# Top-k of a product-key layer: the sums over one-hots move from VectorE to GpSimd, a head behind

## The reference, cut to what matters

```python
s = jnp.einsum('phsd,hsnd->phsn', qry, p['peer_subkeys']).astype(jnp.float32)
s1, i1 = lax.top_k(s[:, :, 0], PEER_TOPK)
s2, i2 = lax.top_k(s[:, :, 1], PEER_TOPK)
cand = (s1[..., :, None] + s2[..., None, :]).reshape(PEER_BLOCK, PEER_HEADS, PEER_TOPK * PEER_TOPK)
cidx = (i1[..., :, None] * PEER_NKEYS + i2[..., None, :]).reshape(PEER_BLOCK, PEER_HEADS, PEER_TOPK * PEER_TOPK)
top_s, pos = lax.top_k(cand, PEER_TOPK)
idx = jnp.take_along_axis(cidx, pos, axis=-1)
gates = jax.nn.softmax(top_s, axis=-1)
```

## Time and profile before

| | |
|---|---|
| median of 3 runs | 4236.36 us (4228.61 to 4244.34) |
| profiled execution, its own time | 4242.22 us |
| its span | 4240.3 us |
| busy over the span | TensorE 3691.2 us (87%), VectorE 3024.4 (71%), ScalarE 1471.0 (35%), GpSimd 2050.7 (48%) |
| mean granted TensorE clock | 0.953 |

### The profile page before, as it was taken

One profiled execution on the slowest core, in us unless ns is written; L12 is line 12 of the kernel. 1 busy time (PEld: TensorE's weight loads), 2 busy tenths in 40 slices (PEclk: granted clock), 3 DMA queues, 4 the chain that ended last, 5 costly groups with the idle time before them and its releaser, 6 DMA issues. The chain is left out here.

```text
span 4240.3 us, 66262 instructions
## 1 busy us (share of the span) xinstructions
PE 3691.2 (87%) x24298; PEld 3423.3 (81%) x24298; DVE 3024.4 (71%) x4791; ACT 1471.0 (35%) x1882; POOL 2050.7 (48%) x1144
## 2 busy tenths in 40 slices
PE   6876999999997898997679999999999898898986
PEld 3335988888896797997578888999898888888886
DVE  4777655566655214898978777778878888888886
ACT  5665444434442113222332332333332322223222
POOL 2333222222224233334047676777777767676772
PEclk9997999999998898998999999999999999999998
DMA  7991222222222123222589999999999999999994
GB/s 301 347 345 66 87 81 85 75 81 79 75 66 100 53 101 114 74 78 92 174 317 401 397 415 396 402 408 418 414 401 405 412 396 418 403 409 416 406 413 169
DMA packets 256208, 1090.68 MB, mean 257 GB/s; under 512 B 25352, under 2 KB 78856, under 8 KB 176392
## 3 DMA queue, kind: packets, MB, share of 16 engines
q1 hardware_dynamic: 170512, 543.60, 34.6%
q0 software_dynamic: 73728, 536.90, 30.9%
q10 hardware_dynamic: 11776, 7.52, 0.6%
HBM read 1047.54 MB, written 40.40 MB: 257 GB/s over the span
## 5 line engine op out<-in xcount | busy, mean ns | idle before, releaser
L248 POOL TENSOR_TENSOR wlo<-raw,whi 128x1024 fp32r<-128x1024 f32 x551 | 1344.4, 2443 | 1333.5 <-ACT whi L244 1328.2
L244 ACT CAST whi<-raw 128x1024 fp32r<-128x1024 f32 x670 | 699.1, 1049 | 1285.2 <-DMA raw<-in_u 535.1
L2099 PE MATMUL gps<-chi,whi 128*128 128x320 f32 x2048 | 656.7, 321 | 110.5 <-DVE outacc L2228 80.9
L263 PE MATMUL gps<-hi_d,whi 128*128 128x320 f32 x2048 | 653.2, 319 | 92.7 <-DVE wlo L253 61.9
L2099 PE MATMUL gps<-chi,wlo 128*128 128x320 f32 x2048 | 645.8, 315 | 0.0
L2099 PE MATMUL gps<-clo,whi 128*128 128x320 f32 x2048 | 645.7, 315 | 0.0
L263 PE MATMUL gps<-lo_d,whi 128*128 128x320 f32 x2048 | 643.6, 314 | 0.0
L263 PE MATMUL gps<-hi_d,wlo 128*128 128x320 f32 x2048 | 643.2, 314 | 0.0
L2186 DVE SCALAR_TENSOR_TENSOR dps<-ring,coef,dps 128x2048 f32<-128x2048 f32 x252 | 591.8, 2348 | 4.7 <-DVE dps L2186 0.9
L2173 DVE CUSTOM_DVE_ANT_0 ring<-ring,dps 128x2048 f32<-128x2048 f32 x256 | 582.2, 2279 | 0.0
L280 PE MATMUL gps<-act_hi,whi 128*128 128x288 f32 x2080 | 477.2, 311 | 37.9 <-POOL act_lo L511 9.0
(11 more groups left out here) (384 smaller groups left out, 5906.6 us busy)
## 6 DMA issues: line engine op xcount, KB each, us to landing
raw<-in_u SPq DMA_DIRECT2D x256, 512.0 KB, 10.5
raw<-in_v SPq DMA_DIRECT2D x256, 512.0 KB, 8.6
wada<-in_w_ada SPq DMA_DIRECT2D x96, 1024.0 KB, 6.6
raw<-in_w_in SPq DMA_DIRECT2D x96, 512.0 KB, 3.4
gateD<-gst SPq DMA_DIRECT2D x8, 2560.0 KB, 9.9
gate<-gateD SPq DMA_DIRECT2D x32, 640.0 KB, 13.5
raw<-in_w_out SPq DMA_DIRECT2D x32, 512.0 KB, 3.7
raw<-in_w_q SPq DMA_DIRECT2D x32, 512.0 KB, 3.8
```

The lines of the kernel that those rows point to most:

```text
L244: act.copy(whi[:, k.slot, :], raw_of(k)).then_inc(W.hi, 1)
L248: pool.tensor_tensor(wlo[:, k.slot, :], raw_of(k), whi[:, k.slot, :].bitcast(F32), ALU.subtract).then_inc(W.lo, 1)
L263: m = pe.matmul(gps[:, bank, 0:DT], w, x[:, kt, :], start=(kt == 0 and n == 0), stop=(kt == KT - 1 and n == 2))
L2099: m = pe.matmul(gps[:, 2 + dt, 0:DT], w[:, slot, cols], x[:, buf, c, :], start=(c == 0 and n == 0), stop=(c == NG - 1 and n == 2))
```

## The change

For heads 0 to 6 VectorE still makes the one-hots, now in one of two tiles (`hots[0]`, `hots[1]`, one for each half), and signals each. GpSimd multiplies them by `topf` and sums over the last axis by halving it: additions of 8, 4, 2 and at last 1 elements out of 16. Each look-up is five instructions; two look-ups a head. They stand in GpSimd's queue two turns later: after the splits (h,1) and (h,3) come the look-ups of head h-2, and those of head 6 come after the splits of head 7 and ahead of the splits of the expert weights. Before VectorE overwrites `topf` it waits for the look-up of the head before. The last head stays on VectorE as it was, and VectorE waits for all 14 look-ups before it makes the expert numbers.

```diff
-        hot = sb("hot", [P, NTT, TOPK, TOPK], at=at5)
+        hots = [sb(f"hot{n}", [P, NTT, TOPK, TOPK], at=at5) for n in range(2)]
...
                 def _(pool):
-                    def body(h):
+                    steps = Chain(pool, S.lsteps, [0])
+
+                    def look_up(h, s):
+
+                        hot = hots[s]
+                        pool.wait_ge(S.hot, h * 2 + s + 1)
+                        steps(pool.tensor_tensor(hot[:, :, :, :], hot[:, :, :, :],
+                                                 bc(topf[:, :, s, :].unsqueeze(2), [P, NTT, TOPK, TOPK]), ALU.mult))
+                        for n in (8, 4, 2):
+                            steps(pool.tensor_tensor(hot[:, :, :, 0:n], hot[:, :, :, 0:n], hot[:, :, :, n:2 * n],
+                                                     ALU.add))
+                        pool.tensor_tensor(slots[:, :, s, h * TOPK:(h + 1) * TOPK], hot[:, :, :, 0], hot[:, :, :, 1],
+                                           ALU.add).then_inc(S.looked, 1)
+
+                    second_h[2](pool)
+                    for h in range(H):
                         for j in range(4):
                             if not prefetched(h, j):
                                 split_lo(pool, wq_half(h, j))
-
-                    second_h[2](pool)
-                    head_turns(pool, body)
+                            if j % 2 and h >= 2:
+                                look_up(h - 2, j // 2)
+                    for s in range(2):
+                        look_up(H - 2, s)
                     for n in range(8 * EARLY + 2):
                         split_lo(pool, Nth(N7 + n))
...
                     def body(h):
+                        last = isinstance(h, int) and h == H - 1
                         for s in range(2):
...
+                            if not isinstance(h, int) or h:
+                                dve.wait_ge(S.looked, h * 2 + (s - 1))
                             dve.tensor_copy(topf[:, :, s, :], topi[:, :, s, :]).then_inc(s_topk[s], 1)
...
-                            ch(dve.tensor_tensor(hot[:, :, :, :], bc(partf[:, s].unsqueeze(3), full),
-                                                 bc(ramp, full), ALU.is_equal))
+                            hot = hots[s]
+                            m = dve.tensor_tensor(hot[:, :, :, :], bc(partf[:, s].unsqueeze(3), full),
+                                                  bc(ramp, full), ALU.is_equal)
+                            if not last:
+                                m.then_inc(S.hot, 1)
+                                continue
+                            ch(m)
...
-                    head_turns(dve, body, ch, 26)
+                    head_turns(dve, body, ch, 20)
+                    dve.wait_ge(S.looked, 2 * H - 2)
```

More of the change, by code:

```diff
@@ L1535, in build @@
             S.early, S.idr, S.x1t, S.x1c, S.x0t = sems(c5, "p5_early", "p5_idr", "p5_x1t", "p5_x1c", "p5_x0t")
+            S.hot, S.looked, S.lsteps = sems(c5, "p5_hot", "p5_looked", "p5_lsteps")
             s_key, s_topk = [S.key0, S.key1], [S.topk0, S.topk1]
```

## The result

The changed kernel takes 4264.49 us (median of 4 runs, 4261.47 to 4265.58), the kernel before 4237.92 us in the same comparison: ratio 1.0058, 95% interval 1.0044 to 1.0072. It is slower by 26.6 us in these medians and by 24.6 us by the ratio; the forecast was slower by 36.5 us, within a range that holds the result.

What follows compares the result with a forecast made beforehand. VectorE was taken as late by about 4 us a head, the last score copy as setting the stage's end. Six 35.3 us periods and a 17.1 us tail put it 37.5 us later: net +36.5, 4273 us, range 4246 to 4308.

Steps and rivals of the forecast that it cites:

- The loop of a head: Middle heads: two splits 4.8, look-up, VectorE's 12.0, look-up, 0.2: 30.6 us without collision; TensorE waits for a split each head.
- VectorE's wait for the look-up: Before VectorE writes topf's second half, it waits some 2 us for GpSimd's look-up of the head before.
- the collision: VectorE's cast and cand additions meet two GpSimd splits on the shared port, losing nearly all of 4.85 us a head.
- L: Time of one GpSimd look-up of five instructions, 2480 elements: 6.8 us, bounds 6.3 to 9.3, 14 times.
- The rival of slow short runs: GpSimd slower on short runs and repeated operands than on flat rows: 9.3 us a look-up gives 4308; chance 0.17.
- The head period: Time from head to head with collision: 30.6 + 4.85 - 0.1 = 35.3 us, against 32.6 to 35.9 before.
- The tail: From head 6's first look-up to the last scores: look-up, splits, load, rounding, copies, signals, 17.1 us; scores 37.5 us later.
- 71.5 - 1: Stage ends 71.5 us after the last score copy; the 1.06 us ScalarE waits for the soft-max today go.
- The low bound: Look-up 6.3 us and no collision, head 29.7 us: last scores at 1942.5, +7 us, 4243.
- The rival without collisions: VectorE's cast and additions get in ahead of the splits: head 30.6 us, +13 us, 4249; chance 0.15.
- The rival of cheap look-ups: Look-up 3.4 us, head about 29 us, TensorE's pace: -3 us, 4233; chance 0.05.
- It is the copy of the last scores that has to come earlier: End of the stage: it ends 71.5 us after ScalarE's last score copy, so only an earlier copy brings a gain.

Runs made afterwards that it cites:

- Run 3: Changed kernel, but GpSimd waits until VectorE has made cand before the first split of heads 3 to 7: 4238.34 us, ratio 0.9994 to the kernel before.
- run 4: Changed kernel, but each look-up leaves out its three middle additions, so sums are incomplete: 4231.81 us, ratio 0.9982 to the kernel before.
- run 5: Changed kernel, but in each head GpSimd does all four splits before the two look-ups: 4243.96 us, ratio 1.0016 to the kernel before.
- Run 1: Changed kernel, but ScalarE copies the last scores before rounding the next two expert halves: 4252.58 us, ratio 1.0035 to the kernel before.
- runs 6 and 7: Changed kernel, last scores before rounding, two expert halves split before last look-ups; plus four splits first per head (4232.93 us) or splits waiting for cand (4231.43 us).
- runs 8 and 9: As the previous two kernels, but four expert halves instead of two split before head 6's look-ups: 4217.27 us (four splits first), 4217.05 us (wait for cand).

## Why the prediction was right, and what it mis-sized

- **Direction and mechanism: right.** The loop of a head was in the trace as described: VectorE's wait for the look-up (1.95 us in the mean, "some 2"), the cast and cand against the two splits, the second comparison ahead of the multiply, TensorE's wait for the split. In runs 3, 4 and 5 the period fell to between 28.1 and 29.6 us. Run 3 broke one link alone, the collision; run 4 took the collision away together with the length of the look-ups, and run 5 together with VectorE's wait.
- **The length of a look-up: a little too long.** L was taken as 6.8 us and is 6.5. The flat rows priced it well: runs of 8, 4 and 2 elements and a repeated operand cost nothing that shows. 640, 320 and 160 elements take 1546, 857 and 452 ns in the mean, where 2.18 ns an element and 0.18 us give 1575, 878 and 529. The rival of slow short runs fell with it.
- **The head period: 35.3 forecast, 33.8 measured.** Split at the look-ups: from the end of look-up (h-2,0) to that of (h-2,1) 11.0 us (11.6 forecast), from there to the next 22.8 (23.7 forecast). Two shorter look-ups account for 0.7 of the 1.5 us. Of the rest, 0.2 is the two splits between the look-ups (4.57 us from the end of one to the start of the next, not 4.8), 0.4 the way from VectorE's release to its first comparison (1823.33 to 1836.91, 13.6 us for 13.95, its collision 4.3 us and not 4.85), and 0.3 the two comparisons, which start 1.40 us apart and not 1.5, and the hold of the multiply behind them. From the end of look-up (0,0) to that of look-up (6,0) it makes 198.5 us instead of 207.0: **8.5 us of the 11 that I was too high**, and the term that was mis-sized.
- **The tail: 17.1 us forecast, 15.9 measured** (1943.12 to 1959.04), 1.2 us less: look-up (6,1) took 6.3 us and not 6.8, the splits and the load 0.2 us less each, the last rounding, copies and signals 0.3 us less. The early products and the last splits after it took 69.6 us, 0.9 less than 71.5 - 1; 0.7 of that lies before the first product, which came 15.3 us after the last scores and not 16.0. Look-up (0,0) ended 42.0 us after the first top-16, not 42.5. In sum 8.5 + 1.2 + 0.9 + 0.5 = 11.1, and 36.5 - 11.1 = 25.4, which is the stage. All four differences point the same way, so the forecast didn't come near by errors that cancel.
- **Two smaller slips.** VectorE's last head ended its sums 29.8 us after the last scores and not 25, since its two multiplies met splits (3.57 and 3.55 us); the soft-max came at 2014.86, so it cost nothing. The low bound took a period of 29.7 us where its own terms give 29.6, which moves that bound by 0.6 us.
- **The rival without collisions** gave +13 us. The changed kernel's rows decide it: GpSimd's split starts 0.07 or 0.08 us ahead of the cast in all five heads that have one there. Run 3, which takes the collisions out, came out 20 us below the changed kernel, in the stage 5 us above the kernel before. The rival of cheap look-ups gave -3 us; run 4, the kernel nearest to it, was faster than that: 9.6 us in the stage.
- **"It is the copy of the last scores that has to come earlier" was only half of the tail.** Run 1 made it 24 us earlier and gained 12: the split that the first product needs stood behind the same look-ups. The sum wasn't touched, since in the changed kernel both came together. My expectations for runs 6 to 9 were: the waits that remained took 5 to 8 us of the gain that I expected in runs 6 and 7, and 2 to 4 us of the 10 to 12 in runs 8 and 9.

The Trainium skill (SBUF — State Buffer, two separate sides) says that of a VectorE and a GpSimd instruction that need the shared port pair the one that starts first has it for its whole length. The trace agrees: the multiply, started 0.16 us after the comparison, shows 4.15 us instead of 2.95, and the other way round the cast shows 2.39 us instead of 0.21.

## What to carry to other kernels

Work moved to an engine with idle time is not free if that engine's queue feeds others in order: write down, for each moved instruction, who is queued behind it and who waits for that, to the last load and copy. Here 43 us of instructions taken from VectorE, the engine that the others waited for in these heads, cost 25 us, and the same instructions in other places of the same queues gave back 44 us. On VectorE and GpSimd, look also at which instructions that hold each other up are released by the same signal: letting the short ones go first (an added wait of 1.3 us a head) was worth 20 us.

## What the runs showed of the hardware that I had not expected

A cast of 80 uint32 elements on VectorE, with one input, is held up by GpSimd as a two-input addition is: 2.39 us against a split and 2.77 us against a look-up's multiply (run 5), 0.21 us alone. TENSOR_REDUCE, with one input too, is not: 1.48 or 1.49 us at every place in both kernels, the one at 1743.53 in the kernel before included, where GpSimd's splits ran until 1745.74.

Time held up hides what is saved: VectorE's busy time fell by 16 us only, where 43 us of instructions were taken away. The casts of topf and the additions of cand alone show 32 us more in the changed kernel than before (49 and 17 us), with the same instructions.
